# Gate one-hots made by one VectorE comparison, with the multiplication by the gate and part of the copies moved to ScalarE

## The chip, the core and the metric

The kernel runs on one core of a Trainium2 chip. The metric is the device time of one execution in microseconds (us). TensorE (PE in the profile) multiplies matrices, VectorE (DVE) and ScalarE (ACT) work element by element, GpSimd (POOL) and SyncE (SP) mostly issue transfers here. Every engine has its own program, carried out in order; the programs meet only at semaphores.

## What is computed

Two transformer blocks follow each other on 256 tokens of width 1024. Each ends in a "PEER" layer: for every token 8 heads choose 16 experts each out of 16384 (128 x 128), and the layer is a gated sum over the chosen experts.

```python
top_s, sel = lax.top_k(cand_s, PEER_TOPK)
idx = jnp.take_along_axis(cand_i, sel, axis=-1)      # 128 experts a token, as i1 * 128 + i2
gates = jax.nn.softmax(top_s, axis=-1)
...
a = jax.nn.gelu(jnp.einsum('cd,chkd->chk', xc, u)) * wc
return jnp.einsum('chk,chkd->cd', a, expert_v[ec])
```

## The kernel before

For 224 of the 256 tokens (T) no expert is gathered: the kernel multiplies the tokens with all 16384 rows of `peer_u`, takes the gelu, multiplies by a dense matrix of gates that is zero where an expert was not chosen, and multiplies with all rows of `peer_v`. The other 32 tokens go by gathers on the side.

**The u stage.** `peer_u` comes as 128 tiles (j = 0 to 127) of 128 x 1024, twice (blk 0 and 1). Each tile lands in a ring of four buffers. ScalarE copies it to `WH` (line 1223, the high part of an fp32 number in fp32r), VectorE subtracts (line 1691) and writes the rest to `WL`. Both are written two tiles ahead, in the helper `fill`: in iteration j each engine prepares tile j + 2. TensorE then needs products of high with high, high with low and low with high (lines 533 to 535, three matmuls for each of 8 pieces k of a tile). ScalarE applies the gelu to the tile's sums (lines 1520, 1522 and, where no gates are ready, 1525).

**The gates.** From tile 83 on the choice of experts is known. It lies in `GIT` with tokens along the free axis: row 0 the gate, rows 1 and 2 the two halves of the expert's number, for 128 chosen experts on the partitions. A group q of four tokens (56 groups, NQ) needs for each token a 128 x 128 one-hot of the first half, `OH[:, i, 0, t]`, and a 128 x 128 one-hot of the second half times the gate, `OH[:, i, 1, t]`, with i = q % 2 (two buffers). TensorE multiplies the two (`gates(q)`, line 892, eight instructions for four fp32 products) into one of four PSUM banks: that is the gate matrix of the four tokens. `SLOTS` fixes at which piece k of which tile this happens: 57 places in tiles 84 to 127, one in most tiles, two in 13 of them, with numbers q = 0 to 56 (q = 56 does nothing on TensorE).

**The order on each engine**, which is written out by hand. In iteration j of tiles 84 to 127:

- ScalarE: `fill` (line 1223, wants a landed tile and a free buffer); for each place q of the tile `one_hots` of group q + 1; then it waits for TensorE's last matmul of tile j (`s_used`) and does the gelu of tile j. Its `one_hots` is four Abs(iota - number) with the number as a per-partition pointer (line 1475) and one Relu(1 - x) over all 512 columns (line 1478).
- VectorE: `fill` (line 1691, wants `s_hi`, that is ScalarE's copy of the same iteration); for each place q `one_hots(q + 1)`, four comparisons with iota that also multiply by the gate (line 2108); then `gated(q - 1, j)`: the first j rows of the gate matrix times the gelus already there (line 2118), the rest copied to `PG` (line 2119); once in a tile `times(j - 1)`, the gates times the gelu of the tile before (line 2126).
- TensorE: the matmuls of tile j with `gates(q)` in between; `gates(q)` waits for both halves of the one-hots (`s_ov` of VectorE, `s_oa` of ScalarE) and, from q = 4 on, for a free bank (`s_gm`).

In iteration 83 both engines make the one-hots of group 0, and in iteration 126 the second place makes none, since all 56 groups have theirs. So in tiles 84 to 126 there are 31 iterations that make one group and 12 that make two; iteration 127 makes none. SyncE loads tiles as the ring comes free; the gathers on GpSimd touch none of this.

Of the kernel before, what the change touches and what calls it, by code (L numbers as in the profile page):

```python
# [8 lines left out]
ALU = mybir.AluOpType  # L9
ACT = mybir.ActivationFunctionType  # L10
# [11 lines left out]
NK = 128  # L22
# [6 lines left out]
NQ = T // 4  # L29
# [63 lines left out]
SLOTS = u_slots()  # L93
SLOT0 = [sum(len(a) for a in SLOTS[:j]) for j in range(NK + 1)]


def gated_before(j):

    return max(SLOT0[j + 1] - 1, 0)
# [126 lines left out]
def two_block_kernel(nc, smalls, consts, fg1, fg2, cr1, cr2, x, wm1, wr1, win1, wf, wpool, wout1, wq1, sk1, u1, ur1, v1,  # L226
                     wr2, win2, wsb, wdil, wout2, wq2, sk2, u2, ur2, v2, out):
    with ExitStack() as ctx:
# [4 lines left out]
        def sem(name):  # L233
            return ctx.enter_context(nc.semaphore(name))
# [13 lines left out]
        GIT = sb("GIT", [128, 3, S])  # L248
        OH = sb("OH", [128, 2, 2, 4, 128])
# [5 lines left out]
        PB = [ctx.enter_context(nc.psum_tensor(f"PB{i}", [128, 512], F32)) for i in range(8)]  # L255
# [40 lines left out]
        s_ge, s_gx, s_eq, s_em, s_gi, s_gtr, s_git = (  # L296
            sem("s_ge"), sem("s_gx"), sem("s_eq"), sem("s_em"), sem("s_gi"), sem("s_gtr"), sem("s_git"))
        s_ov, s_oa, s_gp, s_gm, s_act, s_tm = (
            sem("s_ov"), sem("s_oa"), sem("s_gp"), sem("s_gm"), sem("s_act"), sem("s_tm"))
        s_pair = sem("s_pair")  # L300

        s_hr, s_hc, s_hd, s_pk, s_sx, s_sel = sem("s_hr"), sem("s_hc"), sem("s_hd"), sem("s_pk"), sem("s_sx"), sem("s_sel")
        s_gb = [sem(f"s_gb{i}") for i in range(N_BUF)]
# [23 lines left out]
        iota = KC[:, K_IOTA:K_IOTA + 128]  # L327
# [50 lines left out]
        PG = ar(4096, NK, T)  # L378
# [152 lines left out]
        def tensor_program(e):  # L531
# [123 lines left out]
            for a in range(2):  # L655
                tok = slice(128 * a, 128 * a + 128)
                for k in range(KT):
                    r = three(PB[5][:, 16 * a:16 * a + 16], HH[:, k, tok], HL[:, k, tok], wh[:, k, :], wl[:, k, :],
                              k == 0, k == KT - 1)
            r.then_inc(s_used, 1)  # L660
            for c in range(4):
# [7 lines left out]
                if c == 1:  # L669
                    e.wait_ge(s_fo, 1)  # L670
                    e.wait_ge(s_band, 16)
                    for a in range(2):
                        r = e.matmul(PB[5][:, 0:256], FO[:, a, :], triF[:, a, :], start=a == 0, stop=a == 1)
# [3 lines left out]
            for g in range(4):  # L677
                for a in range(2):
                    r = e.matmul(PB[3 + g // 2][:, 256 * (g % 2):256 * (g % 2) + 256], uT[:, a, 128 * g:128 * g + 128],
                                 band[:, a, g, :], start=a == 0, stop=a == 1)  # L680
                if g % 2:
                    r.then_inc(s_pool, 1)
            for c in range(4):
# [7 lines left out]
                if c == 1:  # L691
# [3 lines left out]
                    for g in range(4):  # L695
# [4 lines left out]
                        for j in range(2):  # L700
                            r = e.matmul(PB[(3, 4, 5, 1)[g]][:, 256 * j:256 * j + 256], w[:, g, 128 * j:128 * j + 128],
                                         poT[:, g, :], start=True, stop=True)
# [144 lines left out]
            def peer(blk, n_q, n_u, n_v, h0):  # L847
# [17 lines left out]
                for c in range(8):  # L865
                    if c < 3:
                        half(1 + c, 0, n_q + 2 * c, h0 if c == 0 else None)
                        half(1 + c, 1, n_q + 2 * c + 1)
                        if c == 0:
                            for k in range(KT):  # L870
                                r = e.transpose(PB[4 + k // 4][0:SP, 128 * (k % 4):128 * (k % 4) + 128], HT[:, k, T:S],
                                                ident)
# [12 lines left out]
                def gates(q):  # L885
                    b, i = 4 + (3 + q) % 4, q % 2
                    if q >= 4:
                        e.wait_ge(s_gm, NQ * blk + q - 3)
                    e.wait_ge(s_ov, NQ * blk + q + 1)
                    e.wait_ge(s_oa, NQ * blk + q + 1)  # L890
                    for t in range(4):
                        r = e.matmul(PB[b][:, 128 * t:128 * t + 128], OH[:, i, 0, t, :], OH[:, i, 1, t, :],  # L892
                                     start=True, stop=True)
                    r.then_inc(s_gp, 1)

                for j in range(NK):
                    n = n_u + j
# [9 lines left out]
                    q = SLOT0[j]  # L907
                    k0 = 0
                    for k in range(KT):
                        due = k in SLOTS[j]  # L910
                        if due or k == KT - 1 or (j, k) in ((JG - 1, 3), (NK - 1, 3)):
                            if WIDE[j]:
                                for m in range(KT):
                                    if m == 0:
                                        e.matmul(both_parts(b), wh[:, m, :], dense(m), start=True, stop=False)
                                    r = e.matmul(PB[b][:, 0:T], wl[:, m, :], HH[:, m, 0:T], start=False, stop=False)  # L916
# [30 lines left out]
                    return e.matmul(PB[c][:, 0:T], lo(n_v + n)[:, cs], HH[:, k, 0:T], start=False, stop=stop)  # L947

                e.wait_ge(s_gm, NQ * (blk + 1))
                for n in range(NK - NW):  # L950
                    e.wait_ge(s_al, NK * blk + n + 1)
                    tile_ready(e, n_v + n)
                    for c in (0, 4, 5, 6, 7, 1, 2, 3):
                        if n == 0 and c == 1:
                            e.wait_ge(s_act, NK * (blk + 1))
                            e.wait_ge(s_tm, times_done(blk, NK - 1))
                        r = weighted(c, n, n == 0, False)
                    r.then_inc(s_used, 1)
# [22 lines left out]
                for c in range(KT):  # L981
                    for n in range(NK - 1 if c < 2 else NK - NW, NK):
                        r = weighted(c, n, False, n == NK - 1)
# [227 lines left out]
        def scalar_program(e):  # L1211
            own = Own(e, s_a)
# [233 lines left out]
            def peer(blk, n_q, n_u, n_v, gelu, gate):  # L1446
# [19 lines left out]
                def one_hots():  # L1466
                    nonlocal q_next
                    q = q_next
                    q_next += 1
                    i = q % 2  # L1470
                    e.wait_ge(s_git, 3 * blk + 2)
                    if q >= 2:
                        e.wait_ge(s_gp, NQ * blk + q - 1)
                    for t in range(4):
                        n = own.mark(e.activation(OH[:, i, 0, t, :], iota, ACT.Abs, scale=-1.0,  # L1475
                                                  bias=GIT[:, 1, 4 * q + t:4 * q + t + 1]))
                    own.done(n)
                    e.activation(OH[:, i, 0, :, :], OH[:, i, 0, :, :], ACT.Relu, scale=-1.0, bias=1.0).then_inc(s_oa, 1)

                def stage(n):  # L1480

# [4 lines left out]
                for j in range(NK):  # L1486
                    if j and WIDE[j - 1]:
                        e.wait_ge(s_used, n_u + j)
                        copy(PG[:, j - 1, :], PB[1 + (7 + j) % 3][:, T:2 * T], s_part)
                    fill(n_u + j)  # L1490
                    if j and WIDE[j - 1]:
                        e.wait_ge(s_sum, added(blk, j - 1))
                        e.activation(PG[:, j - 1, :], PG[:, j - 1, :], gelu).then_inc(s_act, 1)
                    for _ in range(choose_steps(j)):
                        step += 1
                        if step in CHOSEN:
                            a = CHOSEN[step]
                            g = GI[:, 0, a, :].rearrange("p (h k) -> p h k", h=8)
                            e.wait_ge(s_ge, 2 * blk + a + 1)
                            e.activation(g, g, ACT.Exp).then_inc(s_gx, 1)  # L1500
                    if j == JG - 1:
                        one_hots()
                    for _ in SLOTS[j]:
                        if q_next < NQ:
                            one_hots()
                    if WIDE[j]:
                        continue
                    G = 4 * gated_before(j)
                    b = 1 + (8 + j) % 3
                    if j == NK - 1:  # L1510
                        e.wait_ge(s_ufree, blk + 1)
                        e.wait_ge(s_gm, NQ * (blk + 1))
                        stage(0)
                        stage(1)
                    e.wait_ge(s_used, n_u + j + 1)
                    if j >= 80:
                        e.wait_ge(s_git, 3 * blk + 3)
                        e.wait_ge(s_pk, blk + 1)
                    if G:
                        r = e.activation(PB[b][:, 256:256 + G], PB[b][:, 0:G], gelu)  # L1520
                        if G < T:
                            r = e.activation(PG[:, j, G:T], PB[b][:, G:T], gelu)
                        r.then_inc(s_act, 1)
                    else:
                        e.activation(PG[:, j, :], PB[b][:, 0:T], gelu).then_inc(s_act, 1)
# [155 lines left out]
        def vector_program(e):  # L1681
# [405 lines left out]
            def peer(blk, n_q, n_u, n_v, gate):  # L2087
# [13 lines left out]
                def one_hots(q):  # L2101
                    i = q % 2

                    if q >= 2:
                        e.wait_ge(s_gp, NQ * blk + q - 1)
                    for t in range(4):
                        c = 4 * q + t
                        r = e.tensor_scalar(OH[:, i, 1, t, :], iota, GIT[:, 2, c:c + 1], GIT[:, 0, c:c + 1],  # L2108
                                            ALU.is_equal, ALU.mult)
                    r.then_inc(s_ov, 1)  # L2110

                def gated(q, n):

                    ps = PB[4 + (3 + q) % 4][:, :].rearrange("p (r n) -> p n r", r=4)
                    pg = PG[:, :, 4 * q:4 * q + 4]
                    e.wait_ge(s_gp, NQ * blk + q + 1)
                    e.wait_ge(s_act, NK * blk + n)
                    e.tensor_tensor(pg[:, 0:n, :], ps[:, 0:n, :], pg[:, 0:n, :], ALU.mult)
                    e.tensor_copy(pg[:, n:NK, :], ps[:, n:NK, :]).then_inc(s_gm, 1)

                def times(j):
                    G = 4 * gated_before(j)
                    if j >= 0 and G:
                        e.wait_ge(s_act, NK * blk + j + 1)
                        e.wait_ge(s_gm, NQ * blk + gated_before(j))
                        e.tensor_tensor(PG[:, j, 0:G], PB[1 + (8 + j) % 3][:, 256:256 + G], PG[:, j, 0:G],
                                        ALU.mult).then_inc(s_tm, 1)

# [467 lines left out]
```

## Time and profile before

| what | value |
|---|---|
| time, median of 3 runs | 2073.73 us (2073.66 to 2074.74) |
| the profiled execution's own time | 2071.58 us |
| its span, first to last instruction | 2069.8 us |
| TensorE busy in the span | 1989.3 us, 96% |
| VectorE busy | 1688.6 us, 82% |
| ScalarE busy | 1255.4 us, 61% |
| mean granted TensorE clock | 0.989 |

The profile lists for every instruction its engine, line, start and duration, and what ended the idle time before it. The two stages in which gates are made lie at 515 to 694 us and at 1553 to 1732 us of the span. The end of a matmul is modelled, and consecutive matmuls overlap, so busy time of TensorE says that it had work, not how fast it did it.

### The profile page before, as it was taken

What the parts mean: (1) busy time and instruction counts of PE and PEld (TensorE: products, weight loads), DVE (VectorE), ACT (ScalarE), POOL (GpSimd) and SP (SyncE); (2) the same over time, 40 slices, a digit from 0 to 9 for tenths busy, and PEclk for the clock granted to TensorE, in tenths of its full rate; (3) what the DMA queues carried; (4) which work ended last, traced back from release to release, by engine and by line L of the source; (5) the groups of instructions that cost most, each with busy time, mean ns of one, the idle gap of its engine ahead of it and who ended that gap; (6) DMA issues with size and microseconds to landing.
All of it is one profiled execution on the core that took longest, in us unless ns stands there. A gap on an engine that the chain in (4) does not pass through costs nothing.

```text
span 2069.8 us, 37734 instructions
## 1 busy us (share of the span) xinstructions
PE 1989.3 (96%) x14228; PEld 1881.7 (91%) x14228; DVE 1688.6 (82%) x3550; ACT 1255.4 (61%) x2369; POOL 366.7 (18%) x290
## 2 busy tenths in 40 slices
PE   7999999999999999999989998999999999999997
PEld 5998999999999999989879898999999999999997
DVE  3777669999888888989778655699998888888886
ACT  3355655666999655545455454466668996555554
POOL 0000000404100133444100000004041001434340
PEclk9999999999999999999989999999999999999999
DMA  9765566666444699999766533666665345999994
GB/s 376 253 213 170 188 193 199 214 201 201 169 133 132 217 343 377 358 351 359 264 219 249 205 113 103 197 199 214 199 199 176 130 133 199 330 326 326 321 320 142
DMA packets 125156, 476.51 MB, mean 230 GB/s; under 512 B 13808, under 2 KB 14320, under 8 KB 120112
## 3 DMA queue, kind: packets, MB, share of 16 engines
q1 hardware_dynamic: 99168, 362.86, 51.9%
q0 software_dynamic: 20704, 80.55, 10.3%
q10 hardware_dynamic: 5104, 30.69, 3.9%
q8 instruction: 114, 1.87, 0.4%
q14 instruction: 66, 0.54, 0.1%
HBM read 472.14 MB, written 1.05 MB: 229 GB/s over the span
## 4 chain that ended last, share of the span: by engine, by line
PE 63%; DVE 20%; DMA 6%; ACT 5%; issue 4%; POOL 2%; ACTq 0%; DVEq 0%
PE PB L946 13%; PE PB L533 8%; PE PB L535 8%; PE PB L534 8%; DVE WL L1691 8%; PE PB L947 6%; DMA RING<-in_v 5%; PE PB L892 5%; PE PB L918 5%; PE PB L916 3%; ACT WH L1223 2%; PE PB L842 2%; POOL AR L2453 2%; DVE AR L1716 1%; DVE AR L2001 1%
## 5 line engine op out<-in xcount | busy, mean ns | idle before, releaser
L1691 DVE TENSOR_TENSOR WL<-RING,WH 128x1024 fp32r<-128x1024 f32 x651 | 800.8, 1231 | 251.9 <-ACT WH L1223 250.2
L1223 ACT ACTIVATE WH<-RING 128x1024 fp32r<-128x1024 f32 x651 | 686.8, 1056 | 392.9 <-PE PB L947 204.0
L946 PE MATMUL PB<-HX,WH 128*128 128x448 f32 x2048 | 647.1, 376 | 11.7 <-DVE WL L1691 10.5
L947 PE MATMUL PB<-HX,WL 128*128 128x224 f32 x2048 | 538.8, 263 | 0.0
L946 PEld LDWEIGHTS PB<-HX,WH 128*128 128x128 f32 x2048 | 383.7, 187 | 46.2 <-issue 16.0
L533 PE MATMUL PB<-HX,WH 128*128 128x224 f32 (+1 forms) x1360 | 394.8, 290 | 10.3 <-DVE HX L1770 5.7
L947 PEld LDWEIGHTS PB<-HX,WL 128*128 128x128 f32 x2048 | 390.2, 191 | 0.0
L535 PE MATMUL PB<-HX,WL 128*128 128x224 f32 (+1 forms) x1360 | 381.0, 280 | 0.0
L534 PE MATMUL PB<-HX,WH 128*128 128x224 f32 (+1 forms) x1360 | 381.0, 280 | 0.0
L918 PE MATMUL PB<-HX,WH 128*128 128x448 f32 x1162 | 375.4, 375 | 0.0
L916 PE MATMUL PB<-HX,WL 128*128 128x224 f32 x1328 | 326.0, 266 | 0.0
L533 PEld LDWEIGHTS PB<-HX,WH 128*128 128x128 f32 x1360 | 263.4, 194 | 15.7 <-issue 8.8
L534 PEld LDWEIGHTS PB<-HX,WH 128*128 128x128 f32 x1360 | 263.4, 194 | 0.2
L535 PEld LDWEIGHTS PB<-HX,WL 128*128 128x128 f32 x1360 | 263.3, 194 | 0.0
L916 PEld LDWEIGHTS PB<-HX,WL 128*128 128x128 f32 x1328 | 252.7, 190 | 4.3
L918 PEld LDWEIGHTS PB<-HX,WH 128*128 128x128 f32 x1162 | 218.6, 188 | 15.5
L2464 POOL DMA_INDIRECT AR<-in_ur,SPX x64 | 115.2, 1799 | 523.2 <-DVE DOT L2145 516.5
L1227 ACT ACTIVATE AR<-PB 128x224 f32<-128x224 f32 (+4 forms) x251 | 95.8, 391 | 143.3 <-PE PB L918 66.9
L2464 POOL DMA_INDIRECT AR<-in_v,SPX x64 | 133.6, 2088 | 169.5 <-DVE AR L2154 144.4
L1475 ACT ACTIVATE OH<-KC,GIT 128x128 f32<-128x128 f32 x448 | 142.1, 393 | 4.5 <-DVE GIT L2079 4.5
L892 PE MATMUL PB<-OH 128*128 128x128 f32 x896 | 122.0, 279 | 9.1 <-DVE OH L2108 5.7
L2108 DVE TENSOR_SCALAR OH<-KC,GIT 128x128 f32<-128x128 f32 x448 | 124.5, 344 | 0.1
(264 smaller groups left out, 2620.8 us busy)
## 6 DMA issues: line engine op xcount, KB each, us to landing
RING<-in_u SPq DMA_DIRECT2D x256, 512.0 KB, 3.9
RING<-in_v SPq DMA_DIRECT2D x256, 512.0 KB, 6.2
RING<-in_win SPq DMA_DIRECT2D x90, 512.0 KB, 4.3
AR<-in_wr ACTq DMA_DIRECT2D x24, 1024.0 KB, 7.4
RING<-in_wq SPq DMA_DIRECT2D x32, 512.0 KB, 3.6
AR<-in_wr POOLq DMA_DIRECT2D x12, 1024.0 KB, 5.1
AR<-in_wm SPq DMA_DIRECT2D x8, 1024.0 KB, 16.0
RING<-in_wout SPq DMA_DIRECT2D x16, 512.0 KB, 3.5
```

The costliest lines, as they stand in the source:

```text
L533: e.matmul(o, ah, bh, start=start, stop=False)
L534: e.matmul(o, ah, bl, start=False, stop=False)
L535: return e.matmul(o, al, bh, start=False, stop=stop)
L892: r = e.matmul(PB[b][:, 128 * t:128 * t + 128], OH[:, i, 0, t, :], OH[:, i, 1, t, :], start=True, stop=True)
L916: r = e.matmul(PB[b][:, 0:T], wl[:, m, :], HH[:, m, 0:T], start=False, stop=False)
L918: r = e.matmul(both_parts(b), wh[:, m, :], dense(m), start=False, stop=m == KT - 1)
L946: e.matmul(both_parts(c), hi(n_v + n)[:, cs], dense(k), start=start, stop=False)
L947: return e.matmul(PB[c][:, 0:T], lo(n_v + n)[:, cs], HH[:, k, 0:T], start=False, stop=stop)
L1223: e.activation(hi(t), raw(("w", t), words(t)), ACT.Copy).then_inc(s_hi, 1)
L1475: n = own.mark(e.activation(OH[:, i, 0, t, :], iota, ACT.Abs, scale=-1.0, bias=GIT[:, 1, 4 * q + t:4 * q + t + 1]))
L1691: e.tensor_tensor(lo(t), raw(("w", t), words(t)), hi(t).bitcast(F32), ALU.subtract).then_inc(s_lo, 1)
L2464: e.indirect_dma_start(out=GB[:, M % N_BUF, :], out_offset=None, in_=ur if m < GK else v, in_offset=bass.IndirectOffsetOnAxis(ap=SPX[:, 0, ...
```

## The change

VectorE's `one_hots` becomes a single comparison of 1024 columns: iota, repeated over both halves and four tokens, against rows 1 and 2 of `GIT`, each number repeated along 128 columns. It gives both one-hots, neither multiplied by the gate. ScalarE's `one_hots` waits for that comparison (`s_ov`) and multiplies the second one-hot by the gate, four activations of 128 columns with the gate as a per-partition scale. In `gated`, VectorE keeps only the product; the copy of the other rows moves to ScalarE's new `gates_kept`, which waits for that product (`s_gm`) and signals a new semaphore, `s_gc`. `gates(q)`'s wait for a free bank, `times`, and TensorE's start of the next stage wait for `s_gc` accordingly.

```diff
 # TensorE
                 def gates(q):
                     if q >= 4:
-                        e.wait_ge(s_gm, NQ * blk + q - 3)
+                        e.wait_ge(s_gc, NQ * blk + q - 3)
...
                 e.wait_ge(s_gm, NQ * (blk + 1))
+                e.wait_ge(s_gc, NQ * (blk + 1))
...
 # ScalarE
                     i = q % 2
-                    e.wait_ge(s_git, 3 * blk + 2)
-                    if q >= 2:
-                        e.wait_ge(s_gp, NQ * blk + q - 1)
+                    e.wait_ge(s_ov, NQ * blk + q + 1)
                     for t in range(4):
-                        n = own.mark(e.activation(OH[:, i, 0, t, :], iota, ACT.Abs, scale=-1.0,
-                                                  bias=GIT[:, 1, 4 * q + t:4 * q + t + 1]))
-                    own.done(n)
-                    e.activation(OH[:, i, 0, :, :], OH[:, i, 0, :, :], ACT.Relu, scale=-1.0, bias=1.0).then_inc(s_oa, 1)
+                        r = e.activation(OH[:, i, 1, t, :], OH[:, i, 1, t, :], ACT.Copy,
+                                         scale=GIT[:, 0, 4 * q + t:4 * q + t + 1])
+                    r.then_inc(s_oa, 1)
+
+                def gates_kept(q, n):
+
+                    e.wait_ge(s_gm, NQ * blk + q + 1)
+                    e.activation(PG[:, n:NK, 4 * q:4 * q + 4],
+                                 PB[4 + (3 + q) % 4][:, :].rearrange("p (r n) -> p n r", r=4)[:, n:NK, :],
+                                 ACT.Copy).then_inc(s_gc, 1)
...
-                    for _ in SLOTS[j]:
+                    for n in range(len(SLOTS[j])):
+                        q = SLOT0[j] + n
                         if q_next < NQ:
                             one_hots()
+                        if q:
+                            gates_kept(q - 1, j)
...
 # VectorE
-                    for t in range(4):
-                        c = 4 * q + t
-                        r = e.tensor_scalar(OH[:, i, 1, t, :], iota, GIT[:, 2, c:c + 1], GIT[:, 0, c:c + 1],
-                                            ALU.is_equal, ALU.mult)
-                    r.then_inc(s_ov, 1)
+                    e.tensor_tensor(OH[:, i, :, :, :], iota.unsqueeze(1).unsqueeze(1).to_broadcast([128, 2, 4, 128]),
+                                    GIT[:, 1:3, 4 * q:4 * q + 4].unsqueeze(3).to_broadcast([128, 2, 4, 128]),
+                                    ALU.is_equal).then_inc(s_ov, 1)
...
-                    e.tensor_tensor(pg[:, 0:n, :], ps[:, 0:n, :], pg[:, 0:n, :], ALU.mult)
-                    e.tensor_copy(pg[:, n:NK, :], ps[:, n:NK, :]).then_inc(s_gm, 1)
+                    e.tensor_tensor(pg[:, 0:n, :], ps[:, 0:n, :], pg[:, 0:n, :], ALU.mult).then_inc(s_gm, 1)
...
                 def times(j):
-                        e.wait_ge(s_gm, NQ * blk + gated_before(j))
+                        e.wait_ge(s_gc, NQ * blk + gated_before(j))
```

## Rows read from the trace of the kernel before

**Rows 1.** The page: span, and busy time of three engines.
```profile
span 2069.8 us, 37734 instructions
PE 1989.3 (96%) x14228; PEld 1881.7 (91%) x14228; DVE 1688.6 (82%) x3550; ACT 1255.4 (61%) x2369; POOL 366.7 (18%) x290
```

**Rows 2.** Busy time of the engines in the two gate stages.
```profile
core 0: us, PE busy (x) PEld busy (x) DVE busy (x) ACT busy (x) POOL busy (x), PEclk, DMA share, GB/s
515.00:690.60 175.60, 171.06 (x1495) 168.34 (x1494) 155.48 (x421) 159.31 (x411) 5.39 (x7) 1.00 0.44 144
1552.60:1728.00 175.40, 170.87 (x1493) 168.14 (x1492) 155.46 (x420) 159.11 (x411) 5.48 (x7) 1.00 0.44 144
```

**Rows 3.** Waits in 515 to 694 us: total, times, longest.
```profile
DVE WL L1691 <- ACT WH L1223: 19.8, 42, 1.7
ACT PB L1520 <- PE PB L535: 12.3, 35, 0.4
PE PB L892 <- DVE OH L2108: 2.8, 7, 0.4
```

**Rows 4.** Timeline of ScalarE over one iteration with one group (start, duration).
```profile
602.64 1.06 ACT L1223 ACTIVATE WH<-RING 128x1024 fp32r<-128x1024 f32 x1
603.60 1.27 ACT L1475 ACTIVATE OH<-KC,GIT 128x128 f32<-128x128 f32 x4
604.89 0.63 ACT L1478 ACTIVATE OH<-OH 128x512 f32<-128x512 f32 x1
605.91 0.24 ACT L1520 ACTIVATE PB<-PB 128x108 f32<-128x108 f32 x1 [0.39 <-PE PB L535]
606.07 0.26 ACT L1522 ACTIVATE AR<-PB 128x116 f32<-128x116 f32 x1
606.22 1.06 ACT L1223 ACTIVATE WH<-RING 128x1024 fp32r<-128x1024 f32 x1
```

**Rows 5.** Timeline of VectorE over the same iteration.
```profile
603.74 1.23 DVE L1691 TENSOR_TENSOR WL<-RING,WH 128x1024 fp32r<-128x1024 f32 x1 [0.47 <-ACT WH L1223]
604.88 1.11 DVE L2108 TENSOR_SCALAR OH<-KC,GIT 128x128 f32<-128x128 f32 x4
605.91 0.59 DVE L2118 TENSOR_TENSOR AR<-PB,AR 128x420 f32<-128x420 f32 x1
606.41 0.24 DVE L2119 COPY AR<-PB 128x92 f32<-128x92 f32 x1
606.57 0.25 DVE L2126 TENSOR_TENSOR AR<-PB,AR 128x104 f32<-128x104 f32 x1
```

**Rows 6.** Timeline: start of the first gate stage, and its last high part.
```profile
518.27 1.12 DVE L2108 TENSOR_SCALAR OH<-KC,GIT 128x128 f32<-128x128 f32 x4
519.79 0.34 ACT L1525 ACTIVATE AR<-PB 128x224 f32<-128x224 f32 x1
520.03 1.05 ACT L1223 ACTIVATE WH<-RING 128x1024 fp32r<-128x1024 f32 x1
...
690.62 1.06 ACT L1223 ACTIVATE WH<-RING 128x1024 fp32r<-128x1024 f32 x1
```

**Rows 7.** Lines elsewhere: least/median/greatest duration in ns, first and last start.
```profile
L2050 DVE TENSOR_TENSOR AR<-AR,KC x8: 1214/1340/1467, 389.4 to 1539.1; 128x1024 f32<-128x1024 f32 x8
L1280 ACT ACTIVATE AR<-X,ST x3: 1148/1148/1152, 13.2 to 1273.5; 128x1024 f32<-128x1024 f32 x3
L1500 ACT ACTIVATE AR<-AR x4: 311/312/312, 367.7 to 1514.8; 128x128 f32<-128x128 f32 x4
```

**Rows 8.** TensorE in stretches of 2 us: busy time, granted clock, DMA.
```profile
24.00:26.00 2.00, 0.54 (x5) 1.00 1.03 410
38.00:40.00 2.00, 0.51 (x2) 0.70 0.40 160
40.00:42.00 2.00, 2.00 (x11) 0.50 0.81 221
...
46.00:48.00 2.00, 2.00 (x20) 1.00 1.02 428
```

More of the change, by code:

```diff
@@ L299, in two_block_kernel @@
             sem("s_ov"), sem("s_oa"), sem("s_gp"), sem("s_gm"), sem("s_act"), sem("s_tm"))
-        s_pair = sem("s_pair")
+        s_pair, s_gc = sem("s_pair"), sem("s_gc")
         s_hr, s_hc, s_hd, s_pk, s_sx, s_sel = sem("s_hr"), sem("s_hc"), sem("s_hd"), sem("s_pk"), sem("s_sx"), sem("s_sel")
```

## The prediction

> **What bounds the kernel now.** I read the page's busy times first [rows 1]: TensorE is busy 96% of the span, so only a stretch where another engine makes it wait, or would, can change the time. The change touches two stretches, and the busy times by stage show them [rows 2]: in each stage of 175.6 and 175.4 us TensorE is busy 171 us at full clock, ScalarE 159 and VectorE 155. All three are nearly full, but the limit is TensorE: it idles 4.5 us in a stage, and the list of waits [rows 3] puts 2.8 of these on VectorE's one-hots. The other two wait for each other and for TensorE: VectorE 19.8 us for ScalarE's high parts, ScalarE 12.3 us for the last matmul of a tile. The two stages are alike in every number of [rows 2], so I work out one and double it.
>
> The timelines then show the rhythm that matters [rows 4, 5]. From one high part on ScalarE (602.64) to the next (606.22) an iteration takes 3.58 us. Within it VectorE's subtraction starts at 603.74, just as ScalarE's high part has ended (602.64 + 1.06 = 603.70). It always comes right behind it, 42 times in the stage [rows 3]. Then the engines part: ScalarE makes its half of the one-hots while VectorE subtracts and compares. Neither needs the other until the next high part. At the end of the iteration ScalarE has 0.39 us left to wait for TensorE. This is the slack: the loop is set by TensorE and not by the other two.
>
> The high parts of tiles 84 to 127's iterations start at 520.03 and 690.62 [rows 6], so these 43 iterations, from the first start to the last, take 170.6 us now. That is the number to compare with.
>
> **The change, summed as work.** VectorE, per group: four comparisons take 1.11 us [rows 5]. The new one compares 1024 columns with both operands repeated, a form that line 2050 shows at 1.21 us at its fastest and 1.47 at its slowest [rows 7]; I take 1.22, since the subtraction of as many columns shows 1.23 in this very stage [rows 5], and GpSimd, with 5.4 us busy in all [rows 2], leaves VectorE alone there. Dropping line 2119's copy saves 0.16 us (606.41 to 606.57). VectorE thus loses about 0.05 us per group, which is nothing. ScalarE, per group: it had four Abs and a Relu, from 603.60 to 604.89 + 0.54 = 605.43 (0.63 less the 0.09 or so by which consecutive records overlap: 602.64 + 1.06 is 0.10 past 603.60). The four multiplications carry one per-partition pointer each, as the Abs did. A pointer scale makes 1024 columns 1.15 us (line 1280) where the plain copy of line 1223 takes 1.06, and a plain 128-column activation takes 0.31 (line 1500) [rows 4, 7]; 0.31 + 0.09 is 0.40, the Abs's own (1.27 for four that start 0.29 apart: 3 x 0.29 + 0.40). So 4 x 0.29 = 1.17 us. The kept copy reads 4 x (128 - j) columns of PSUM, 176 down to 4, on average some 88; line 1520 advances 0.16 us for 108 columns, so I take 0.14. ScalarE falls from 1.84 to 1.31 us per group, by 0.5.
>
> The Trainium skill, VectorE: DVE Perf Modes, the section on the trn2 errata, says that an SBUF-source instruction pays a fixed cost each time and that few wide ones beat many narrow ones, and gives (N + 151)/0.96 ns for an fp32 tensor_tensor, 1224 ns at 1024 columns. The duration agrees with line 2050's fastest; the profit doesn't come, since the wide one carries twice the columns of the four it replaces. By that page alone both engines get lighter or stay, and the sum would be no loss.
>
> **The change, summed as a chain.** Work is not what decides. ScalarE now may not multiply before VectorE has compared, VectorE compares behind its own subtraction, the subtraction needs ScalarE's high part of the same iteration, and ScalarE reaches the next high part only after the multiplications. Everything that ran side by side stands in one ring. Queued behind ScalarE's wait on `s_ov` are the kept copy, the gelu and the next high part; VectorE's next subtraction waits for that one. There is no way round it inside the written order: the high part that could keep VectorE fed is behind the wait. From high part to high part, with one group:
>
> - high part to the start of the subtraction: 603.74 - 602.64 = 1.10; the neighbouring iterations also give 1.08 and 1.09; I take 1.09
> - subtraction to the start of the comparison: 604.88 - 603.74 = 1.14
> - comparison to its end, and over to ScalarE: 1.22 + 0.04 (the 603.70 to 603.74 of above)
> - four multiplications 1.17, kept copy 0.14
> - both gelus: 606.22 - 605.91 = 0.31
>
> Sum 5.11 us, against 3.58 now. `gates_kept` also waits for VectorE's product, but that ends 0.51 us behind the comparison (0.59 less the 0.08 by which VectorE's records overlap: 603.74 + 1.23 is 0.09 past 604.88), well inside the 1.17 of the multiplications: it costs nothing here. The comparison's wait for a free `OH` buffer is met an iteration earlier. TensorE needs 3.58 us for its share of an iteration, gates included, so it waits for one-hots some 1.5 us in each, and the last matmul of a tile is always done when the gelu wants it: that wait goes to zero.
>
> An iteration with two groups adds, between the first and the second comparison's start, the first comparison's 1.14 (as the subtraction's), the product's 0.50 (605.91 to 606.41) and `times`, 0.25 less 0.08 overlap, 0.16: 1.80 us. The first multiplications and the first kept copy, 1.31, lie beside these. So 6.91 us.
>
> 31 x 5.11 + 12 x 6.91 = 158.4 + 82.9 = 241.3 us, less the 170.6 of now: 70.7 us. At the start, ScalarE's group 0 must wait for the comparison: 518.27 + 1.22 + 0.04 + 1.17 + 0.24 (the gelu of line 1525 up to the high part, 519.79 to 520.03) = 520.94 instead of 520.03, 0.9 us more [rows 6]. Behind the last iteration the order is that of before (subtraction, last product, stage of the next tiles), and I price it at nothing. Per stage 71.6 us, for both 143.2. The profiled execution took 2071.58 us of its own time, 1.8 beyond its span and 2.2 under the median of the runs; I set the sum on the median: 2073.7 + 143.2 = 2217 us, 6.9% slower.
>
> **Bounds.** Comparison: at 1.47 it adds 0.25 on each of 55 groups per stage, +28 us for both. Downward, a product of about 512 columns takes 0.6 to 0.7; were the comparison as cheap as 0.7, -57 us; I hold that for far off, as 1024-column instructions of every kind in rows 5 and 7 take 1.2, and let the range take in half. Multiplications: without any cost of the pointer 0.22 apart, -0.3 on each of 43 iterations, -25 us; if they don't overlap at all (0.39 each) +0.4, +34. Kept copy: 0.06 to 0.35, as its access is scattered by four, -7 to +18. No single end brings the ring below 3.58 us: all low ends together leave 5.11 - 0.52 - 0.30 - 0.08 = 4.2.
>
> **The rivals.**
>
> (A) *The work decides, not the chain: no change.* It asks that VectorE and ScalarE stay an iteration apart, so that the comparison is done when ScalarE asks. For it speak the summed busy times, which fall. Against it speaks that the subtraction starts 0.04 us behind each high part [rows 3 to 5]: VectorE has no lead, and can't get one. Time: 2074. The Trainium skill, Perfetto Trace Analysis, section on the most-contended engine, would judge by occupancy; neither of the two lighter engines is the fullest, so it too would give no change.
>
> (B) *The idle time of TensorE goes: faster.* The same condition, and the lighter engines deliver one-hots earlier. All idle time of both stages is 9 us [rows 2], so at best 2065. It decides from the point where the ring is under 3.58 us; it is priced at 5.11.
>
> (C) *The clock falls too: slower still.* TensorE would be busy only 70% of the stage. In the trace a stretch of 2 us with 1.46 idle kept the full clock (24 to 26), another with 1.49 idle went to 0.70 and then to 0.50, the half clock of 1.2 GHz, though the engine was then busy; it was full again at 46 [rows 8]. At half clock an iteration's matmuls take 7.1 us, over the ring's 5.11. Some 6 us at half clock let TensorE do 3 us of work where 4.2 are due, so an episode costs 1.2 us; one every 12 us would make 40 episodes and 48 us: 2265. The Trainium skill, TensorE: Matmul & The Clock Gate, its rules on why this matters for kernels, warns of idle gaps between bursts of matmuls; the rows at 38 to 42 agree, those at 24 to 26 show that a gap of this size need not do it.
>
> **How the numbers follow.** The chain, with its bounds, 0.83; C 0.11; A 0.03; B 0.03. Predicted 2217. The likeliest case alone reaches from 2190 to 2250; with part of C the range is 2190 to 2260. A time within 0.2% of before, about what a measurement of this kernel can tell from no change, comes only from A; slower by more is 0.94.
>
> **What would show it.** In the profile after: high parts 5.1 us apart with one group and 6.9 with two; ScalarE's line of the multiplication waiting some 2.4 us for VectorE's comparison in each iteration (1.09 + 1.14 + 1.22 + 0.04, less the 1.06 of the high part); no wait of the gelu for TensorE; TensorE waiting for ScalarE's `OH` about 1.5 us in each tile, some 70 us a stage; VectorE idle before its subtraction longer than before, with less busy time on both; the comparison at 1.22 us; the granted clock near 1.0. If the multiplication finds its comparison ready, the chain is wrong and A or B holds. If the clock in the stages stands under 0.9, C does.

## The result, and the profile after

The changed kernel takes 2218.56 us (median of 4 runs, 2216.26 to 2220.84) against 2073.69 for the one before (4 runs): a ratio of 1.0703, with a 95% interval of 1.0687 to 1.0719. That is 144.9 us more; 143.2 were forecast.

The page of the kernel after: span, busy times, the slices of the granted clock, and the chain that ended last.

```profile
span 2219.0 us, 37180 instructions
PE 2041.4 (92%) x14228; PEld 1926.3 (87%) x14228; DVE 1683.5 (76%) x3102; ACT 1206.2 (54%) x2369; POOL 369.8 (17%) x290
PEclk9999999999998999999999999999999989999999
PE 46%; DVE 26%; ACT 14%; issue 8%; DMA 5%; POOL 2%; DVEq 0%; ACTq 0%
```

VectorE and ScalarE are busy for less time than in [rows 1], 5 and 49 us less, and the kernel is 7% slower. Neither engine is short of time. The list of waits of the first gate stage says what takes it (total, times, longest):

```profile
ACT OH L1474 <- DVE OH L2114: 113.1, 56, 3.9
DVE WL L1699 <- ACT WH L1224: 94.5, 45, 2.5
PEld PB L892 <- issue: 34.8, 22, 2.2
PE PB L892 <- ACT AR L1481: 32.5, 23, 2.0
PEld PB L892 <- ACT AR L1481: 24.0, 16, 2.1
PE PB L892 <- ACT OH L1474: 20.1, 15, 2.0
```

ScalarE waits 113 us of a stage for VectorE's comparison, once for every group, and VectorE 94 us for ScalarE's high part, against 19.8 in [rows 3]. Each waits for the other for two fifths of the time: a ring. TensorE's wait is its consequence: its matmuls (the two PE rows) wait 53 us together. The two PEld rows are the weight loads of the same matmuls, so they show the same waits a second time. The waits put on line 1481, the kept copy, are for ScalarE's multiplications of line 1474, since `gates(q)` needs no kept copy as late as that one; the copy is only the event that came last.

ScalarE's timeline of one iteration with one group, and of one with two:

```profile
644.57 1.04 ACT L1224 ACTIVATE WH<-RING 128x1024 fp32r<-128x1024 f32 x1
648.04 1.28 ACT L1474 ACTIVATE OH<-OH,GIT 128x128 f32<-128x128 f32 x4 [2.43 <-DVE OH L2114]
649.22 0.22 ACT L1481 ACTIVATE AR<-PB 128x88 f32<-128x88 f32 x1
649.34 0.24 ACT L1528 ACTIVATE PB<-PB 128x112 f32<-128x112 f32 x1
649.53 0.25 ACT L1530 ACTIVATE AR<-PB 128x112 f32<-128x112 f32 x1
649.67 1.04 ACT L1224 ACTIVATE WH<-RING 128x1024 fp32r<-128x1024 f32 x1
653.14 1.28 ACT L1474 ACTIVATE OH<-OH,GIT 128x128 f32<-128x128 f32 x4 [2.43 <-DVE OH L2114]
...
654.97 1.28 ACT L1474 ACTIVATE OH<-OH,GIT 128x128 f32<-128x128 f32 x4 [0.42 <-DVE OH L2114]
...
656.60 1.04 ACT L1224 ACTIVATE WH<-RING 128x1024 fp32r<-128x1024 f32 x1
```

From high part to high part it is 5.10 us with one group (644.57 to 649.67), where [rows 4] had 3.58, and 6.93 with two (649.67 to 656.60). The wait before the first multiplication is 2.43 us, the number worked out ahead. In both iterations the two gelus (lines 1528, 1530) follow with no wait for TensorE, where [rows 4] had 0.39. The 43 iterations of the stage go from 521.39 to 763.29, 241.9 us; 241.3 were forecast, from 170.6. In the second stage they take 242.9 us (1634.37 to 1877.30).

### The profile page after: what moved, and what is told of

Its sections match the earlier page's. It is cut to its first block, busy times and chain, and to the rows that moved or that the text cites. A ratio compares the mean times of both kernels' runs of the same rounds, so it can differ in the third digit from the quotient of the medians.

```text
span 2219.0 us, 37180 instructions
## 1 busy us (share of the span) xinstructions
PE 2041.4 (92%) x14228; PEld 1926.3 (87%) x14228; DVE 1683.5 (76%) x3102; ACT 1206.2 (54%) x2369; POOL 369.8 (17%) x290
## 4 chain that ended last, share of the span: by engine, by line
PE 46%; DVE 26%; ACT 14%; issue 8%; DMA 5%; POOL 2%; DVEq 0%; ACTq 0%
PE PB L946 13%; DVE WL L1699 8%; PE PB L947 6%; DVE OH L2114 6%; ACT WH L1224 5%; PE PB L533 5%; PE PB L534 4%; PE PB L535 4%; ACT OH L1474 4%; DMA RING<-in_v 4%; PE PB L918 4%; POOL AR L2458 2%; PE PB L916 2%; PE PB L842 2%; DVE AR L1724 1%
## 5 line engine op out<-in xcount | busy, mean ns | idle before, releaser
L946 PEld LDWEIGHTS PB<-HX,WH 128*128 128x128 f32 x2048 | 383.8, 187 | 49.1 <-issue 18.2
L533 PE MATMUL PB<-HX,WH 128*128 128x224 f32 (+1 forms) x1360 | 413.0, 304 | 10.4 <-DVE HX L1778 5.7
L534 PE MATMUL PB<-HX,WH 128*128 128x224 f32 (+1 forms) x1360 | 397.9, 293 | 0.0
L535 PE MATMUL PB<-HX,WL 128*128 128x224 f32 (+1 forms) x1360 | 397.1, 292 | 0.0
L947 PEld LDWEIGHTS PB<-HX,WL 128*128 128x128 f32 x2048 | 390.2, 191 | 0.0
L533 PEld LDWEIGHTS PB<-HX,WH 128*128 128x128 f32 x1360 | 281.2, 207 | 15.1 <-issue 8.7
L534 PEld LDWEIGHTS PB<-HX,WH 128*128 128x128 f32 x1360 | 281.3, 207 | 0.2
L535 PEld LDWEIGHTS PB<-HX,WL 128*128 128x128 f32 x1360 | 280.2, 206 | 0.0
L1474 ACT ACTIVATE OH<-OH,GIT 128x128 f32<-128x128 f32 x448 | 143.2, 390 | 226.1 <-DVE OH L2114 226.1
L916 PEld LDWEIGHTS PB<-HX,WL 128*128 128x128 f32 x1328 | 252.7, 190 | 4.2
L918 PEld LDWEIGHTS PB<-HX,WH 128*128 128x128 f32 x1162 | 218.6, 188 | 15.4
L892 PE MATMUL PB<-OH 128*128 128x128 f32 x896 | 130.5, 291 | 104.1 <-ACT AR L1481 64.2
L892 PEld LDWEIGHTS PB<-OH 128*128 128x128 f32 x896 | 113.2, 198 | 116.7 <-issue 69.2
```

Source lines behind the costliest of these rows:

```text
L533: e.matmul(o, ah, bh, start=start, stop=False)
L534: e.matmul(o, ah, bl, start=False, stop=False)
L535: return e.matmul(o, al, bh, start=False, stop=stop)
L918: r = e.matmul(both_parts(b), wh[:, m, :], dense(m), start=False, stop=m == KT - 1)
L946: e.matmul(both_parts(c), hi(n_v + n)[:, cs], dense(k), start=start, stop=False)
L1474: r = e.activation(OH[:, i, 1, t, :], OH[:, i, 1, t, :], ACT.Copy, scale=GIT[:, 0, 4 * q + t:4 * q + t + 1])
```

## The experiments

All are variants of the changed kernel or of the one before, run beside the latter.

### Only the one-hots the new way

```diff
-                        if q:
-                            gates_kept(q - 1, j)
...
                     e.tensor_tensor(pg[:, 0:n, :], ps[:, 0:n, :], pg[:, 0:n, :], ALU.mult)
+                    e.tensor_copy(pg[:, n:NK, :], ps[:, n:NK, :]).then_inc(s_gm, 1)
```

> The changed kernel, but VectorE keeps copying the rest of each gate matrix, as before; only the one-hots are made the new way. Chain theory: the ring high part, subtraction, comparison, multiplications, gelu is 5.11 - 0.14 (no kept copy) = 4.97 us with one group and 4.97 + 1.80 + 0.16 (VectorE's copy between the two comparisons) = 6.93 with two; 31 x 4.97 + 12 x 6.93 = 237 us in place of 170.6, with 0.9 at the start +67.6 a stage, so 2209 us. If the work and not the order decides, about 2074. If the copy's move carries the loss, 2074 too.

Measured: 2210.62 us, ratio 1.0650 (1.0619 to 1.0681). That is 135 us over the kernel before in the runs beside it (2075.61), so the one-hots alone bring 135 of the 145 us. ScalarE's wait before the multiplications is 2.43 us here too.

### The same, with the wait for the comparison taken away

ScalarE's multiplications now read iota, and the waits that take the place of `s_ov` are for `GIT` and for ScalarE's own group before, both met early.

```diff
-                    e.wait_ge(s_ov, NQ * blk + q + 1)
+                    e.wait_ge(s_git, 3 * blk + 2)
+                    if q:
+                        e.wait_ge(s_oa, NQ * blk + q)
                     for t in range(4):
-                        r = e.activation(OH[:, i, 1, t, :], OH[:, i, 1, t, :], ACT.Copy,
+                        r = e.activation(PB[0][:, 128 * t:128 * t + 128], iota, ACT.Copy,
                                          scale=GIT[:, 0, 4 * q + t:4 * q + t + 1])
```

> The kernel of compare_only (copies on VectorE), with ScalarE's multiplications reading iota and writing to an idle PSUM bank, without a wait for the comparison; the gates are left out of the gate matrices. Work per engine as in compare_only, to the instruction. Chain theory: no ring is left but the subtraction behind the high part, TensorE bounds the stage again: 2066 to 2076 us, against 2209 for compare_only. If the wide comparison or the multiplications cost by themselves, it stays near compare_only.

Measured: 2074.88 us, ratio 1.0001 (0.9988 to 1.0015). Both engines carry out as many instructions of the same sizes as in the run before it, and the 135 us are gone. The one difference in price is small: a multiplication that writes to PSUM takes 367 ns in place of 387 (medians), and four still start 0.29 us apart. The first gate stage's waits:

```profile
ACT PB L1527 <- PE PB L535: 49.2, 36, 2.4
DVE WL L1698 <- ACT WH L1223: 14.8, 36, 0.9
PEld PB L892 <- issue: 7.0, 14, 0.6
```

ScalarE's gelu waits for TensorE again, 49 us a stage: the limit is back where it was. This pair shows the cause of the one-hots' part of the loss: not the price of an instruction, but who waits for whom.

### Only the copy moved to ScalarE

The one-hots are those of before; `gates_kept` and `s_gc` are kept from the change.

> The kernel before, but the copy of the rest of each gate matrix moved to ScalarE behind VectorE's product; one-hots as before. The prediction gave the wait on the product no cost, because the multiplications cover it. Here nothing covers it: high part to subtraction 1.09, subtraction 1.14, four comparisons 1.02, product 0.59, over 0.04, kept copy 0.14, gelus 0.31 = 4.33 us with one group, and 1.02 + 0.50 + 0.16 more = 6.01 with two. 31 x 4.33 + 12 x 6.01 = 206 us in place of 170.6: +36 a stage, 2145 us. A ring of its own, hidden in the other. If only the one-hots' order matters, 2074, since ScalarE's 0.14 us more work lies in its idle time.

Measured: 2154.14 us, ratio 1.0378 (1.0337 to 1.0419), so +79 instead of +71 us. ScalarE's timeline around an iteration with one group and one with two:

```profile
641.76 1.05 ACT L1224 ACTIVATE WH<-RING 128x1024 fp32r<-128x1024 f32 x1
...
645.65 0.23 ACT L1484 ACTIVATE AR<-PB 128x76 f32<-128x76 f32 x1 [1.01 <-DVE AR L2129]
...
646.13 1.06 ACT L1224 ACTIVATE WH<-RING 128x1024 fp32r<-128x1024 f32 x1
...
650.04 0.23 ACT L1484 ACTIVATE AR<-PB 128x72 f32<-128x72 f32 x1 [1.02 <-DVE AR L2129]
650.17 1.27 ACT L1476 ACTIVATE OH<-KC,GIT 128x128 f32<-128x128 f32 x4
651.47 0.63 ACT L1479 ACTIVATE OH<-OH 128x512 f32<-128x512 f32 x1
...
652.44 1.05 ACT L1224 ACTIVATE WH<-RING 128x1024 fp32r<-128x1024 f32 x1
```

With one group it is 4.37 us, where 4.33 were forecast. With two it is 6.31 and not 6.01: ScalarE's second set of Abs and Relu (650.17 on, 1.83 us) is queued behind the first kept copy, which waits for the product, and I had let it run beside VectorE's second round. 12 x 0.3 + 31 x 0.04 = 4.8 us a stage, 9.7 for both, takes the sum from 2145 to 2155. The copy's move alone has a ring of its own that costs 79 us; in the changed kernel it lies in the shadow of the other, where it adds some 10 (ratio 1.0703 against 1.0650).

### All the work of the change, without the wait for the comparison

The changed kernel with ScalarE's multiplications edited as two experiments above.

> The changed kernel with all its instructions, but ScalarE's four multiplications read iota and write to an idle PSUM bank, so that they don't wait for VectorE's comparison; the gates are therefore left out of the gate matrices. Chain theory: the comparison's ring is gone, but ScalarE still waits for VectorE's product before the kept copy: 1.09 + 1.14 + 1.14 + 0.59 + 0.04 + 0.14 + 0.31 = 4.45 us with one group, 6.25 with two: 138 + 75 = 213 us, +42 a stage, 2158 us. If the wait for the comparison is all there is, 2074. If the work decides, as the changed kernel, 2218.

Measured: 2155.67 us, ratio 1.0385 (1.0318 to 1.0452). The high parts stand 4.46 us apart with one group and 6.32 with two, in this stretch (6.08 to 6.45 with two over the first stage), from the timeline of ScalarE:

```profile
641.12 1.05 ACT L1224 ACTIVATE WH<-RING 128x1024 fp32r<-128x1024 f32 x1
...
645.12 0.23 ACT L1483 ACTIVATE AR<-PB 128x76 f32<-128x76 f32 x1 [1.82 <-DVE AR L2126]
...
645.58 1.05 ACT L1224 ACTIVATE WH<-RING 128x1024 fp32r<-128x1024 f32 x1
...
651.90 1.05 ACT L1224 ACTIVATE WH<-RING 128x1024 fp32r<-128x1024 f32 x1
```

Forecast were 4.45 and 6.25. The second ring, over the product and the kept copy, takes over as soon as the first is cut. No run has the kept copy without its wait for the product, in which both engines would read the same PSUM bank with nothing to order them. So the second ring is shown by its sum and its wait and by `copy_only`, not by taking its wait away.

### The comparison made twice

```diff
+                    own.done(own.mark(e.tensor_tensor(OH[:, i, :, :, :], ...the same comparison...)))
                     e.tensor_tensor(OH[:, i, :, :, :], iota.unsqueeze(1).unsqueeze(1).to_broadcast([128, 2, 4, 128]),
```

> The changed kernel with VectorE's comparison carried out twice into the same buffer, the second behind the first. Chain theory: every comparison lies on the ring whole, the first and the second of an iteration, so each of the 56 in a stage costs 1.22 + 0.03 us more: 56 x 1.25 x 2 = 140 us over the changed kernel, 2359 us. If the ring has slack or TensorE at the lower clock bounds part of it, less; if VectorE's work decides instead, VectorE, now idle two fifths of the stage, takes it for nothing: 2218.

Measured: 2359.91 us, ratio 1.1384 (1.1354 to 1.1413); 141 us over the changed kernel, where 140 were forecast. VectorE was idle two fifths of the stage and still nothing of the second comparison was hidden. Idle time inside a ring takes no work for free.

### The first comparison ahead of the subtraction

```diff
                 for j in range(NK):
+                    if j >= JG:
+                        if SLOT0[j] + 1 < NQ and SLOTS[j]:
+                            one_hots(SLOT0[j] + 1)
                     if j >= JG - 1:
                         fill(n_u + j)
...
-                        if q + 1 < NQ:
+                        if n and q + 1 < NQ:
                             one_hots(q + 1)
```

> The changed kernel with one step moved: in each iteration VectorE makes the comparison of the first group ahead of its subtraction; products and the second comparison stay behind it. Chain theory: the comparison is off the ring, which now goes over the product: 1.09 + 1.14 + 0.59 + 0.04 + 0.14 + 0.31 = 3.31 us with one group, under TensorE's 3.57, but 1.09 + 1.14 + 0.50 + 0.16 + 1.22 + 0.04 + 1.17 + 0.14 + 0.31 = 5.77 with two, 0.8 over TensorE's 4.96, of which the next iterations win back up to 0.26 each. 2 to 9 us a stage: 2078 to 2092 us. If something other than the written order costs the 145 us, near 2218.

Measured: 2080.84 us, ratio 1.0041 (1.0027 to 1.0056). One step moved on one engine takes 138 of the 145 us back. The high parts stand 3.31 to 3.32 us apart in iterations with one group (600.43, 603.74, 607.06), the product's ring as summed, faster than TensorE can follow for long; the iterations with two groups take 5.68 to 5.91, where 5.77 was forecast. All 43 iterations take 172.3 us in each stage of the profiled execution, 1.7 more than before. That execution was the fastest of eight (2072.95 us, the slowest 2087.18), so where the rest of the median's 8 us lies the trace does not show.

### All gate work ahead of the subtraction, and the same in the kernel before

```diff
                     if j >= JG - 1:
                         fill(n_u + j)                     # now only for j == JG - 1
...
                     if not SLOTS[j]:
                         times(j - 1)
+                    fill(n_u + j)
```

> The changed kernel with all of VectorE's gate work of an iteration (comparisons, products, times) ahead of its subtraction. Chain theory: nothing that ScalarE waits for lies behind its own high part any more; VectorE needs 2.94 us with one group and 4.6 with two, ScalarE 2.6 and 3.9, TensorE 3.57 and 4.96, so TensorE bounds the stage and the 145 us go: 2066 to 2076 us. It beats the kernel before by at most the 4.5 us of TensorE's idle time a stage. If the comparison, the multiplications or the copy cost by themselves, it stays above 2090.

> The kernel before with the same move of VectorE's gate work ahead of its subtraction, and nothing of the change. TensorE bounds the stage before and after the move: 2066 to 2076 us. If groups_first is faster than this one, the change itself is worth something once its order is mended; I expect the two within 4 us of each other.

> The kernel of groups_first once more, beside the other on the same chip: 2056 us, 0.992 of before.

> groups_first with the copy of the rest of each gate matrix back on VectorE: the one-hots are made the new way, the copy the old way. VectorE needs 3.1 us with one group and 4.9 with two, ScalarE 2.4 and 3.6. With two groups VectorE then has 0.06 us left under TensorE's 4.96, against 0.3 in groups_first, and no wait of ScalarE on the product remains. If the rest of groups_first's gain over before_groups_first comes from VectorE's lighter load, this one lies between the two, 2056 to 2061 us; if the copy's wait on ScalarE costs anything still, it is faster than groups_first.

| kernel | median us | ratio to before |
|---|---|---|
| groups_first | 2055.98 | 0.9917 (0.9901 to 0.9934) |
| groups_first_again | 2055.79 | 0.9921 (0.9907 to 0.9936) |
| compare_only_groups_first | 2054.98 | 0.9913 (0.9895 to 0.9931) |
| before_groups_first | 2061.06 | 0.9940 (0.9926 to 0.9954) |

With its order mended the change is 17 us faster than the kernel before, some 160 us faster than as written, and 5 us faster than the old one-hots in the same order. So 12 of the 17 us come from the order alone, and only 5 from the change. That the copy lies on ScalarE or on VectorE makes no difference that could be measured. All forecasts of these runs were too high: 2066 to 2076 for groups_first and for before_groups_first, with at most 4 us between them, and 2056 to 2061 for compare_only_groups_first. I had bounded the gain by TensorE's idle time, 9 us in all. The timelines of an iteration with two groups show where it comes from. ScalarE in the kernel before:

```profile
554.08 1.06 ACT L1223 ACTIVATE WH<-RING 128x1024 fp32r<-128x1024 f32 x1
555.02 1.27 ACT L1475 ACTIVATE OH<-KC,GIT 128x128 f32<-128x128 f32 x4
556.33 0.63 ACT L1478 ACTIVATE OH<-OH 128x512 f32<-128x512 f32 x1
556.87 1.26 ACT L1475 ACTIVATE OH<-KC,GIT 128x128 f32<-128x128 f32 x4
558.16 0.63 ACT L1478 ACTIVATE OH<-OH 128x512 f32<-128x512 f32 x1
558.70 0.19 ACT L1520 ACTIVATE PB<-PB 128x48 f32<-128x48 f32 x1
...
559.02 1.05 ACT L1223 ACTIVATE WH<-RING 128x1024 fp32r<-128x1024 f32 x1
```

groups_first, the same tile:

```profile
555.63 1.06 ACT L1224 ACTIVATE WH<-RING 128x1024 fp32r<-128x1024 f32 x1
...
559.50 0.19 ACT L1528 ACTIVATE PB<-PB 128x48 f32<-128x48 f32 x1
...
559.83 1.04 ACT L1224 ACTIVATE WH<-RING 128x1024 fp32r<-128x1024 f32 x1
```

Before, this iteration took 4.94 us without a wait anywhere on ScalarE (0.94 + 2 x 1.84 + 0.32 = 4.94). Six of the twelve iterations with two groups are like it; the other six take 5.24 or 5.25, with a wait of 0.23 us for TensorE before the gelu. With the change it takes 4.20 here, and the one behind it 3.84; in others it is 4.46 and 3.58. Both pairs make 8.04, which is TensorE's pace. TensorE's true share of an iteration with two groups is therefore 4.46, and I had read 4.96 out of the kernel before. What TensorE did there is shown by its matmuls around the wait, and by VectorE's comparison that ends just before them (start, duration):

```profile
556.31 1.11 DVE L2108 TENSOR_SCALAR OH<-KC,GIT 128x128 f32<-128x128 f32 x4
...
556.92 0.27 PE L534 MATMUL PB<-HX,WH 128*128 128x224 f32 x1
557.03 0.27 PE L535 MATMUL PB<-HX,WL 128*128 128x224 f32 x1
557.52 1.13 PE L892 MATMUL PB<-OH 128*128 128x128 f32 x8 [0.21 <-issue]
558.41 0.35 PE L533 MATMUL PB<-HX,WH 128*128 128x224 f32 x1
```

Matmuls start 0.11 us apart but their records last 0.27. The stop from 557.03 to 557.52 is 0.38 us over the rhythm, and shows as 0.21 idle. It ends 0.10 us behind VectorE's comparison (556.31 + 1.11 = 557.42), which stood behind VectorE's subtraction and so behind ScalarE's high part: the kernel before had the written order's cost already. Measured from the start of one matmul to the start of the next and added up over the first gate stage, the gate products from the second group on start 7.1 us late in the kernel before, 2.0 in before_groups_first and 0.1 in groups_first. The 43 iterations take 170.6, 165.2 and 162.6 us. So the order alone takes most of the stops away, although ScalarE still needs its 4.94 to 4.96 us in all twelve iterations with two groups: the ones behind them then take 3.11 or 3.45 and win much of it back. The order also takes 1.0 us off the tail behind the last high part. The last 2.6 us a stage go with ScalarE's lighter work, since compare_only_groups_first, where VectorE's is not lighter, stands at 162.6 too; 0.9 of these are given back at the start of the stage, where ScalarE waits for the first comparison. So a stage with its start and tail is 8.0 us shorter than before, 6.4 by the order and 1.6 by the change, and both stages account for 16 of the 17 us.

## Why the prediction was right

**The ring.** It was forecast at 5.11 and 6.91 us; measured are, with one group, 5.04 to 5.18 but for the first and the last iteration of a stage (4.89, and 5.43 or 5.34), and with two 6.80 to 7.09 but for three (7.25, 7.43, 7.89). For the one-hots, cutting the wait with all their work left in place brought the time back to 1.0001 of before; doubling one of the ring's members cost what the member takes. The terms came from rows of the kernel before, and each stood: the comparison 1.22 us (1215 to 1224 ns over 112 of them), the multiplications 1.19 to the kept copy's start, the wait 2.43, the kept copy 0.06 to 0.21 up to the gelu's start, 0.14 forecast. One sign was read too high: TensorE's matmuls wait 53 us a stage by their records and not some 70.

**The product's wait costs nothing.** True where it was said: the multiplications cover it. It was left unsaid that this cover is itself part of the loss. copy_only shows the same wait at 79 us once the multiplications' wait is gone.

**The start of the stage.** 0.9 us forecast. From the first comparison to the high part it is now 518.71 to 521.39 against 518.27 to 520.03 in [rows 6], 0.92 more, and as much in the second stage.

**The tail was priced at nothing.** TensorE's first matmul of the next stage comes 4.74 us behind the last high part (763.29 to 768.03), before 4.20 (690.62 to 694.82): 0.5 us. The first matmuls of tile 127 ran at half clock there, 0.21 us apart. In the second stage the tail is no longer than before (4.09 us against 4.19).

**Rival C, the clock falls too.** The mechanism came, and its price did not. The granted clock in the first gate stage is 0.92 on average, where the prediction had expected near 1.0 and had named under 0.9 as the sign of C. Stretches of 2 us of the kernel after:

```profile
664.00:666.00 2.00, 0.63 (x6) 1.00 0.51 104
666.00:668.00 2.00, 1.41 (x11) 0.88 0.39 158
668.00:670.00 2.00, 2.00 (x11) 0.50 0.01 4
670.00:672.00 2.00, 1.67 (x11) 0.77 0.71 250
```

TensorE idled 1.97 us before 666.59, then worked some 3 us at 1.2 GHz, matmuls 0.21 us apart in place of 0.11. The iteration around it, at a mean clock of 0.75, took 6.95 us (666.79 to 673.74), against 6.89 for one at 1.00 (610.31 to 617.20); iterations with two groups grow by 0.01 to 0.03 us from one to the next over the stage, at either clock. I had charged 1.2 us for each episode, as if TensorE's lag lay on the ring; mostly it lies in the 1.5 us that TensorE waits in each iteration anyway. It is not always so. Where an episode fell late in an iteration with two groups, from its second gate products on, the tile's last matmul could come late and hold up the ring. The worst case is the iteration from 1836.83 to 1844.72, 7.89 us at a mean clock of 0.81, where ScalarE's gelu waits for TensorE:

```profile
1844.41 0.31 ACT L1528 ACTIVATE PB<-PB 128x188 f32<-128x188 f32 x1 [0.80 <-PE PB L535]
```

Five of the 24 iterations with two groups are longer than their neighbours (7.01, 7.09, 7.25, 7.43, 7.89), by some 1.8 us in all, an estimate from the trend of the others; 48 us were C's price. compare_twice, with a mean clock of 0.946 over its whole span, agrees: its sum holds to 1 us without any term for the clock.

**Rival A, no change by lighter work,** fell with the first row of waits: the multiplication found its comparison ready in none of 56 cases. **Rival B, faster,** was right in what it needs, another order, and wrong in its bound: groups_first gains 17 us and not 9, since I took TensorE's idle time, as recorded, for all that could be won. The prediction also says that TensorE and not the other two sets the loop. That holds with one group; with two, TensorE's share is 4.46 us and the kernel before took 4.94 to 5.25. The sum did not suffer, as it goes from the measured 170.6.

The Trainium skill's formula in VectorE: DVE Perf Modes, in the section on the trn2 errata, gave the right duration (1224 ns estimated by it, 1218 measured at the median) and had nothing to say on the order, which decided. Judging by occupancy alone, as the Trainium skill's Perfetto Trace Analysis does in Identifying the Most-Contended Engine, would have called the changed kernel harmless; the runs speak against using it alone here.

What is not settled: the two profiled spans differ by 149.2 us, and the gate stages with their starts and tails make up 145.9 of these. Of the other 3.3 us, 2.8 lie between the two stages, and their cause stays open; runs of the kernel before scatter over 10 us (2067.7 to 2078.0 in 17 runs). That the sum came within 2 us of the medians' difference is therefore in part luck; that it came within 1 to 2 us for the iterations of each stage is not.

## What to carry to other kernels

When a step is split between two engines that run in order and already hand each other something in every iteration, write down the ring: from one hand-over to the same one an iteration later, through every wait. Here its sum against the iteration's length decided, not the busy times, and a wait that is covered today can be a second ring that stands behind the first. Before such a split is given up, move the producer's part ahead of what it is queued behind: here, with all of VectorE's gate work moved so, a loss of 7.0% became a gain of 0.8%. Then give the old kernel the same order before crediting the split: it gained 0.6% by that alone.

## What the runs showed of the hardware

TensorE's busy time overstates its work in this stage, since each record outlasts the distance to the next matmul by 0.16 us; a stop of 0.38 us left 0.21 in the profile. The distance from one start to the next tells more: by it TensorE stopped for 7.1 us in a stage of the kernel before, where [rows 2] leave 4.5 idle. And a TensorE that waits once in each iteration for at most 2.1 us lost its full clock again and again (0.92 on average, single stretches at 0.50), which cost next to nothing (some 1.8 us in all, estimated above) because in most iterations the ring left it more time than the half clock took away.
